# One of the four weight sums of each seven-product set made by an accumulating transfer

## What is computed

```
mixed = jnp.concatenate([o_fox, o_sb, o_ssm, o_lru], axis=-1) @ w_out   # (256 x 4096) @ (4096 x 4096)
return h + rmsnorm(mixed, g_post)
```

## Time and profile before

| | us |
|---|---|
| median of 3 runs | 1507.57 |
| lowest, highest | 1507.29, 1508.12 |
| the profiled execution, its own time | 1507.15 |
| span of its trace, first to last instruction | 1505.4 |

### The profile page before, as it was taken

One profiled execution on the slowest core, in us unless ns is written; L12 is line 12 of the kernel. 1 busy time (PEld: TensorE's weight loads), 2 busy tenths in 40 slices (PEclk: granted clock), 3 DMA queues, 4 the chain that ended last, 5 costly groups with the idle time before them and its releaser, 6 DMA issues.

```text
span 1505.4 us, 21466 instructions
## 1 busy us (share of the span) xinstructions
PE 1494.7 (99%) x7014; PEld 1230.7 (82%) x7014; DVE 1069.0 (71%) x1322; ACT 906.8 (60%) x1229; POOL 99.9 (7%) x148
## 2 busy tenths in 40 slices
PE   8999999999999999999999999999999999999998
PEld 7888888888888888888888888888888888888886
DVE  5665479899888895566555555455547899989977
ACT  6644476666766666666765455476567666656553
POOL 0000020111201110000000101000000000000000
PEclk9999999999999999999999999999999999999999
DMA  8565556565555655566565555554556666655875
GB/s 319 180 196 160 190 168 199 185 196 176 187 188 185 193 175 190 182 192 190 181 226 182 171 168 181 179 182 156 174 171 205 206 227 202 202 198 201 268 246 199
DMA packets 86715, 292.56 MB, mean 194 GB/s; under 512 B 9976, under 2 KB 13312, under 8 KB 86528
## 3 DMA queue, kind: packets, MB, share of 16 engines
q1 hardware_dynamic: 78480, 280.27, 57.7%
q10 hardware_dynamic: 8176, 11.54, 2.3%
HBM read 287.56 MB, written 4.20 MB: 194 GB/s over the span
## 4 chain that ended last, share of the span: by engine, by line
PE 95%; DVE 2%; DMA 1%; issue 1%; ACT 0%; SPq 0%; ACTq 0%; DVEq 0%
PE main L393 24%; PE main L395 24%; PE main L394 24%; PE main L674 3%; PE main L675 3%; PE main L676 3%; PE side L674 2%; PE side L675 2%; PE side L676 2%; DMA w_raw<-in_wall 1%; PE main L434 1%; PE main L580 1%; DVE w_lo L1697 1%; PE side L521 1%; PE main L532 1%
## 5 line engine op out<-in xcount | busy, mean ns | idle before, releaser
L1221 DVE TENSOR_TENSOR w_lo<-w_raw,w_hi 128x1024 fp32r<-128x1024 f32 x407 | 499.6, 1231 | 379.9 <-ACT w_hi L784 378.7
L784 ACT ACTIVATE w_hi<-w_raw 128x1024 fp32r<-128x1024 f32 x407 | 427.4, 1056 | 372.5 <-PE main L395 350.8
L393 PE MATMUL main<-w_hi,acts 128*128 128x512 f32 x1640 | 647.7, 395 | 0.0
L395 PE MATMUL main<-w_hi,acts 128*128 128x512 f32 x1640 | 639.6, 390 | 0.0
L394 PE MATMUL main<-w_lo,acts 128*128 128x512 f32 x1640 | 639.1, 390 | 0.0
L393 PEld LDWEIGHTS main<-w_hi,acts 128*128 128x128 f32 x1640 | 308.2, 188 | 66.1 <-issue 3.7
L395 PEld LDWEIGHTS main<-w_hi,acts 128*128 128x128 f32 x1640 | 308.0, 188 | 64.8
L394 PEld LDWEIGHTS main<-w_lo,acts 128*128 128x128 f32 x1640 | 308.3, 188 | 62.2
L800 ACT ACTIVATE w_hi<-w_raw 128x1024 fp32r<-128x1024 f32 x67 | 70.9, 1061 | 69.1 <-PE side L676 50.1
L1697 DVE TENSOR_TENSOR w_lo<-w_raw,w_hi 128x1024 fp32r<-128x1024 f32 x67 | 81.2, 1221 | 6.8 <-ACT w_hi L800 4.9
L1911 POOL TENSOR_TENSOR scr<-scr 128x256 f32<-128x256 f32 x32 | 28.1, 878 | 438.6 <-ACT scr L889 438.6
(11 more groups left out here) (390 smaller groups left out, 1589.0 us busy)
## 6 DMA issues: line engine op xcount, KB each, us to landing
w_raw<-in_wall SPq DMA_DIRECT2D x463, 512.0 KB, 3.5
scr<-in_wall SPq DMA_DIRECT2D x36, 512.0 KB, 5.6
cross<-in_wall SPq DMA_DIRECT2D x12, 512.0 KB, 5.6
br<-in_x SPq DMA_DIRECT2D x16, 256.0 KB, 7.3
w_raw<-in_wglu SPq DMA_DIRECT2D x8, 512.0 KB, 3.7
out<-br SPq DMA_DIRECT2D x5, 512.0 KB, 2.7
vals<-in_x ACTq DMA_DIRECT2D x8, 256.0 KB, 4.5
br<-in_gpost ACTq DMA_DIRECT2D x8, 256.0 KB, 4.4
```

What stands on the lines that cost most here:

```text
L393: pe.matmul(main[:, bank0 + a, :], u_h, wh, start=(k == 0), stop=False)
L395: mm = pe.matmul(main[:, bank0 + a, :], u_l, wh, start=False, stop=(k == NK - 1))
L784: act.activation(w_hi[:, c % RING, :], w_raw[:, c % RING, :], ACT.Copy).then_inc(hi_ready, 1)
L1221: dve.tensor_tensor(w_lo[:, c % RING, :], w_raw[:, c % RING, :], w_hi[:, c % RING, :].bitcast(F32), ALU.subtract).then_inc(lo_ready, 1)
```

## The change

T1 is no longer made by DVE. A second transfer from DRAM of B11, issued by POOL with an accumulating write (`accum_op=ALU.add`), adds B11 onto B12 in slot 2, after the load of slot 2 has landed. So T1 = B11 + B12, in slot 2 in place of slot 0. A transfer can only add here, so the other signs follow: T2 = B22 + T1 in slot 3, T3 = T2 - B11 (= B22 + B12) in slot 0, T4 = B21 + T2 in slot 1. DVE makes T2 and T3 behind the low tile of B22 and T4 behind that of B21. Some signs in `make_combs` and `shared_sums` turn with it, with no instruction added or taken. ACT and DVE wait for the accumulating transfer on a new semaphore, `t1_in`. The SP queue loads slot 2 ahead of slot 0 in all sets but the first and the last of a pair's order lists (the first set of the first pair keeps 0, 1, 2, 3, and set 7 keeps 2, 3, 0, 1). The added copies of slot 2 in `S_SETS` are 12 in all (3 pairs by 4 sets), 512 KB each.

```diff
 def raw_last_op(t, j):
-    return SET0[t] + ({0: T1, 1: T4, 2: T3, 3: T2}[j] if t in S_SETS else plain_slot(t, j))
+    return SET0[t] + ({0: T3, 1: T4, 2: T1, 3: T2}[j] if t in S_SETS else plain_slot(t, j))
...
-                for j in (0, 1, 2, 3) if p == 0 and t == 0 else (2, 3, 0, 1) if t == SETS - 1 else (0, 2, 3, 1):
+                for j in (0, 1, 2, 3) if p == 0 and t == 0 else (2, 3, 0, 1) if t == SETS - 1 else (2, 0, 3, 1):
...
             def high_pair(m):
-                j = {B11: 0, B22: 3, T1: 0, B21: 1, T3: 2, T2: 3, T4: 1}[i] if t in S_SETS else plain_slot(t, i)
+                j = {B11: 0, B22: 3, T1: 2, B21: 1, T3: 0, T2: 3, T4: 1}[i] if t in S_SETS else plain_slot(t, i)
...
-                if t in S_SETS and i in (T1, T2, T3, T4):
-                    sums = 4 * (p * len(S_SETS) + S_SETS.index(t))
-                    act.wait_ge(t_sum, sums + {T1: 1, T3: 2, T2: 3, T4: 4}[i])
+                if t in S_SETS and i == T1:
+                    act.wait_ge(t1_in, 16 * (p * len(S_SETS) + S_SETS.index(t) + 1))
+                elif t in S_SETS and i in (T2, T3, T4):
+                    sums = 3 * (p * len(S_SETS) + S_SETS.index(t))
+                    act.wait_ge(t_sum, sums + {T2: 1, T3: 2, T4: 3}[i])
...
             def low_pair(m):
...
-                if i == B11:
-                    dve.wait_ge(raw_in[2], 16 * (RAW0 + p * SETS // 2 + t // 2 + 1))
+                if i == B22:
+                    dve.wait_ge(t1_in, 16 * (sums + 1))
                     dve.wait_ge(lo_ready, OPS0 + m + 1)
-                    dve.tensor_tensor(b11, b12, b11, ALU.subtract).then_inc(t_sum, 1)
-                if i == B22:
-                    dve.wait_ge(t_sum, sums + 1)
-                    dve.tensor_tensor(b12, b22, b12, ALU.subtract).then_inc(t_sum, 1)
-                    dve.wait_ge(t_sum, sums + 2)
+                    dve.tensor_tensor(b22, b22, b12, ALU.add).then_inc(t_sum, 1)
+                    dve.wait_ge(t_sum, 3 * sums + 1)
+                    dve.tensor_tensor(b11, b22, b11, ALU.subtract).then_inc(t_sum, 1)
+                if i == B21:
+                    dve.wait_ge(t_sum, 3 * sums + 1)
                     dve.wait_ge(lo_ready, OPS0 + m + 1)
-                    dve.tensor_tensor(b22, b22, b11, ALU.subtract).then_inc(t_sum, 1)
-                if i == B21:
-                    dve.wait_ge(t_sum, sums + 3)
-                    dve.wait_ge(lo_ready, OPS0 + m + 1)
-                    dve.tensor_tensor(b21, b21, b22, ALU.subtract).then_inc(t_sum, 1)
+                    dve.tensor_tensor(b21, b21, b22, ALU.add).then_inc(t_sum, 1)
...
         def _(pool):
...
+            for p in range(N_PAIRS):
+                for n, t in enumerate(S_SETS):
+                    pool.wait_ge(raw_in[2], 16 * (RAW0 + p * SETS // 2 + t // 2 + 1))
+                    c = 2 * t
+                    pool.dma_start(raw_at(t, 2), wall[B_OUT + 1 + 2 * p, :, c * CW:(c + 1) * CW],
+                                   accum_op=ALU.add).then_inc(t1_in, 16)
```

More of the change, by code:

```diff
@@ L266, in hybrid_trunk @@
         raw_x = [sem(f"raw_x{n}") for n in range(RING)]
-        t_sum, p1_out, s_sum, c_sum = sem("t_sum"), sem("p1_out"), sem("s_sum"), sem("c_sum")
+        t_sum, t1_in, p1_out, s_sum, c_sum = (sem(n) for n in ("t_sum", "t1_in", "p1_out", "s_sum", "c_sum"))
         g_in, xl_in = sem("g_in"), [sem("xl_in0"), sem("xl_in1")]
@@ L1629, in make_combs @@
                     dve.wait_ge(comb_lo, done)
-                dve.tensor_tensor(into(0), part(k1, 1), part(k2, 1), ALU.add).then_inc(comb_sum, 1)
+                dve.tensor_tensor(into(0), part(k1, 1), part(k2, 1), ALU.subtract).then_inc(comb_sum, 1)
                 dve.tensor_tensor(into(2), part(k1, 0), part(k1, 1), ALU.subtract).then_inc(comb_sum, 1)
@@ L1634, in make_combs @@
                 dve.wait_ge(comb_sum, done + 3)
-                dve.tensor_tensor(into(3), part(k2, 0), into(1), ALU.subtract).then_inc(comb_sum, 1)
+                dve.tensor_tensor(into(3), part(k2, 0), into(1), ALU.add).then_inc(comb_sum, 1)
             def comb_low(n):
@@ L1700, in low_pair @@
                 b11, b21, b12, b22 = (raw_at(t, n) for n in range(RING))
-                sums = 4 * (p * len(S_SETS) + S_SETS.index(t))
-                if i == B11:
-                    dve.wait_ge(raw_in[2], 16 * (RAW0 + p * SETS // 2 + t // 2 + 1))
+                sums = p * len(S_SETS) + S_SETS.index(t)
+                if i == B22:
+                    dve.wait_ge(t1_in, 16 * (sums + 1))
                     dve.wait_ge(lo_ready, OPS0 + m + 1)
-                    dve.tensor_tensor(b11, b12, b11, ALU.subtract).then_inc(t_sum, 1)
-                if i == B22:
-                    dve.wait_ge(t_sum, sums + 1)
-                    dve.tensor_tensor(b12, b22, b12, ALU.subtract).then_inc(t_sum, 1)
-                    dve.wait_ge(t_sum, sums + 2)
-                    dve.wait_ge(lo_ready, OPS0 + m + 1)
-                    dve.tensor_tensor(b22, b22, b11, ALU.subtract).then_inc(t_sum, 1)
-                if i == B21:
-                    dve.wait_ge(t_sum, sums + 3)
-                    dve.wait_ge(lo_ready, OPS0 + m + 1)
-                    dve.tensor_tensor(b21, b21, b22, ALU.subtract).then_inc(t_sum, 1)
+                    dve.tensor_tensor(b22, b22, b12, ALU.add).then_inc(t_sum, 1)
[3 more added lines that the diff above has]
+                    dve.wait_ge(t_sum, 3 * sums + 1)
+                    dve.wait_ge(lo_ready, OPS0 + m + 1)
+                    dve.tensor_tensor(b21, b21, b22, ALU.add).then_inc(t_sum, 1)
             def low_out(c):
@@ L1756, in shared_sums @@
                 dve.wait_ge(s_sum, 4 * p + 1)
-                dve.tensor_tensor(c12, P5_BANK, c21, ALU.add).then_inc(s_sum, 1)
+                dve.tensor_tensor(c12, P5_BANK, c21, ALU.subtract).then_inc(s_sum, 1)
                 dve.wait_ge(s_sum, 4 * p + 2)
@@ L1760, in shared_sums @@
                 dve.wait_ge(s_sum, 4 * p + 3)
-                dve.tensor_tensor(c22, P5_BANK, c21, ALU.add).then_inc(s_sum, 1)
+                dve.tensor_tensor(c22, P5_BANK, c21, ALU.subtract).then_inc(s_sum, 1)
             def own_sum(p, n, a):
```

## The result

The changed kernel takes **1511.59 us** (median of 7 runs, 1510.76 to 1513.27) against 1507.29 us (7 runs, 1507.02 to 1508.12) for the kernel before on the same chip. The ratio is 1.0029, with a 95% interval of 1.0019 to 1.0039: 4.3 us slower. The forecast was 1509.4 (1.8 us slower), the range 1506.7 to 1513.9. The range held the time only because it reached to the bound of a rival, "slow first transfer", which had a chance of 0.29. The likeliest case was not what happened.

The account below looks back on a forecast made before the run. PE's rate was taken to bound the kernel. A boundary gain of 0.5 us and a first-set delay of 2.3 us made +1.8 us on 1507.57, so 1509.4 us, range 1506.7 to 1513.9.

Parts of the forecast that it names:

- slow first transfer: Rival, chance 0.29: in the first set X is between 7.9 and 11.3 us; time 1510.5 to 1513.9 us.
- The likeliest case: First set late by 1 to 3.4 us, time 1507.6 to 1510.5 us, likeliest 1509.4; chance 0.43.
- The cap of 0.9 us: PE's idle time from 1204 to 1450 us, claimed as the most that relieving DVE could win.
- Part 1: DVE's twelve removed sums: nothing in the first set, 0.25 us at each of two later pair boundaries, 0.5 us gained.
- Part 2: Accumulating transfer in the first set: PE delayed by max(0, X - 4.5), claimed as 2.3 us.
- X: Time from POOL's issue of the accumulating transfer until its semaphore is full; taken as 6.8 us for the first set.
- The 11.3 of the upper bound: Longest X for the first set, in us: the add ends behind the whole burst, then takes 1024 KB.
- The estimate of 4.4 us: Lower figure for X from the skill's pages, with 1024 KB read; the first set's delay would be nil.
- Part 3: Accumulating transfers in the other eleven sets: hidden between early reload and use, costed at nothing.
- slow in every set: Rival, chance 0.09: X over 15 us, each of 12 sets costs X - 15 besides; 1529.6 us at X = 16.
- The limit of 15 us: In the other eleven sets, the X from which PE would begin to wait.
- Part 4: Moved loads on SP's queue, with B11's slot 0 reloaded after T3's low tile: costed at nothing.

Follow-up runs that it names:

- no_sums: Changed kernel with all 48 weight sums left out, 36 of DVE and 12 of the transfers, so the result is not the layer's; 1505.36 us, ratio 0.9986.
- best transfer version: Changed kernel with T1 of only the very first set made by DVE, the other eleven by transfer; 1506.98 us, ratio 0.9994; repeated, 1506.95 us.
- two_pool: Changed kernel with the transfer only in the first set of pairs 2 and 3, the other ten T1 sums on DVE; 1507.69 us, ratio 1.0003.
- plain_pool: Changed kernel with POOL's twelve transfers as plain loads without the add, so the sums are not the layer's; 1509.84 us, ratio 1.0016.
- burst_late: Changed kernel with SP holding the four loads of set 1 until the first accumulating transfer has landed; 1508.43 us, ratio 1.0002.
- hold_b11: Changed kernel with POOL's other eleven transfers held until B11's low tile of their own set; 1568.59 us in one execution.
- all_dve: Changed kernel with all twelve T1 sums given back to DVE, new signs, slots and load order kept; 1508.19 us, ratio 1.0001.
- swap: Changed kernel with B12 loaded into the slot that comes free first in the first set, so POOL issues earlier; 1508.32 us, ratio 1.0003.
- after_again: The changed kernel unchanged, measured again on the same chip; 1511.61 us, ratio 1.0030 against the kernel before.

## Why the prediction was right or wrong

- **PE's rate bounds the kernel and caps the gain:** right in kind. The cap of 0.9 us was too low. Without any weight sum the kernel wins 2.2 us, in good part for the reason given at no_sums: the earlier trace rows names less than a wait costs (0.32 for 0.58 us). The best transfer version won 0.7 to 0.8, not resolved.
- **Part 1, 0.25 us for each boundary:** the place was right, the size was 0.56. My limit of 0.4 us from the freeing of the slot was worked out wrongly. The timeline before has B22's high tile at 1278.34, so its low tile could have begun at 1279.4; it was DVE's own row of work that held it until 1282.34. And two_pool suggests that part of the gain comes from other sets.
- **Part 2, delay = max(0, X - 4.5):** right. With X = 9.54 it gives 5.0; T3's low tile was 4.75 us later, from a transfer issued 0.3 us earlier than I had it (1196.60). Against PE's own start it was 5.29 later: the issue stood 6.96 us ahead of PE's first product and not 7.2. PE's one wait stood at T1, the first product behind that sum; at half clock PE then found B21's and T3's low tiles ready.
- **X = 6.8:** this is the step that failed. I took one argument (sharing with the burst) and another (twice the bytes), which gave the same figure, as two confirmations of it. They are two costs that act at once and nearly add. POOL's least plain transfer took 4.0 us. Sharing alone makes it the 7.59 of plain_pool, the add alone about the 6.55 of burst_late, and both together 8.65 to 9.85, where the plain sum of the two would be 10.1. My own rows gave the hint: in a burst where 512 KB take 6.8 in the median, an add that stands for 1024 KB was not to be expected at 6.8 as well. The prediction's own sign of being wrong, X over 8 us, came true. The 11.3 of the upper bound held: the add landed at 1206.14, before the last of the burst.
- **The estimate of 4.4 us from the Trainium skill** ("DMA: Bandwidth & Descriptors", "Anatomy of one DMA — SWDGE (gpsimd) path", with two source reads): too low by the runs. The least of all adds took 5.3 us, the medians of the kernels with eleven or twelve unheld adds were 6.8 to 7.6, and the one that mattered took 9.5. For a plain transfer of POOL the same fit gives 3.2 us, as an estimate, and the least measured was 4.0.
- **Part 3:** right. No wait in eleven sets, at landings up to 10.1 us. The rival "slow in every set" never had its condition, and the held-back kernels show that it exists. The limit of 15 us itself was tried only in the second set of hold_b11 (3.1 us of wait against 3.3).
- **Part 4, moved loads and signs:** right within 1.5 us, by all_dve. The DMA share rose from 0.64 to 0.73, as forecast. "Nothing by itself" of the added 6 MB was wrong at one place: each plain load of the burst took 3.2 to 3.5 us longer. PE did not wait for them there. In swap ACT waited for the loads beside the transfer.
- **Not foreseen:** the granted clock fell to 0.50 in the wait of 3.5 us.
- **The sum:** with X = 9.54 and the boundaries at 0.56 my own formula gives 5.0 - 1.1 = +3.9 and, with up to 0.7 for the clock, 3.9 to 4.6; measured +4.3. The rival's mechanism named two causes, the first run of POOL's program and the burst. The burst (2 to 3 us of X) is shown, and so is the add itself (1 to 2 us), which the rival did not name. That the first transfer is slow by being first is not shown, beyond 0.15 us of issue; at most about 1 us of it is left open.

## What to carry over

An added transfer has two prices, its own time and what it takes from the loads beside it, so look at each place where it meets a burst and judge it by its worst use, not by its median: eleven of these twelve were free, and one cost more than all could give. Where two effects each explain an unknown duration, ask whether they act at once, and if they do, count both. And before relieving an engine, find out what it is worth by leaving its work out: here it was 2.2 us for all 48 sums.

## What the runs showed of the hardware

- An accumulating transfer of 512 KB from DRAM onto SBUF, issued by POOL, landed 5.3 to 10.1 us after its issue in the kernel after, and took 3.1 us of all 16 engines. Without the add the same queue took 1.9 us and landed in 4.0 to 7.6. For SP's queue it is 57.1% x 1509.7 / 535 = 1.6 us, its 280.27 MB being 535 times 512 KB, and 1.7 in the trace of plain_pool (59.9%).
- Its issue occupied POOL for 0.86 us, the first for 1.01; without the add 0.53 and 0.72 us.
- The add and the burst slowed each other: from 6.55 to 8.65 and up to 9.85 us for the one, and from a median of 6.8 to 10.3 for the other (8.6 beside a plain transfer of POOL).
- Around PE's wait of 3.5 us the granted clock was 0.50 for some 6.8 us, and around the wait of 3.9 us in after_again for some 3.4. In the profiled executions of burst_late, swap and plain_pool, with waits of 0.7 to 1.7 us, it stayed at 1.00. With a wait in nearly every set the clock was low for some 30 to 45 us in all. What that cost, beyond the waits, no run separates.
